# Softmax weights of attention units: broadcast by VectorE and turned, in place of two broadcast matmuls on TensorE

## The chip, the cores and the metric

One core of a Trainium2 chip. The metric is the device time of one execution in microseconds; before: median 2764.86 us of three runs (2764.49, 2764.86, 2767.98). The core's engines are TensorE (PE, its weight loads listed apart as PEld), VectorE (DVE), ScalarE (ACT), GpSimd (POOL) and SyncE (SP). Matmul results land in PSUM, in banks of 512 float32 columns.

## The reference, cut to what matters

Two transformer blocks in float32. The first has two layers over 512 latent and 256 context tokens, each with three attention mixers of 8 heads of width 64: A (global), B (a neighbourhood on a grid) and C (a sliding window with a sink logit per head). The second block has two layers over 512 tokens with, beside other mixers, a causal attention of 4 heads with forget decays. All of them end alike:

```python
def softmax_f32(s, dtype):
    return jax.nn.softmax(s.astype(jnp.float32), axis=-1).astype(dtype)

    def block(qi):
        s = jnp.einsum('bqhgd,bkhd->bhgqk', qi, k_all)
        p = softmax_f32(s, v_all.dtype)
        return jnp.einsum('bhgqk,bkhd->bqhgd', p, v_all)
```

Context tokens attend to context tokens alone, and only in the first layer of block one, since nothing reads them after it.

## The kernel before, in words

Attention works in units. A unit is one block of 128 queries for a pair of heads (e = 0 and 1). There are 136: in layer 0 of block one 16 latent and 8 context units for each of A, B and C, in layer 1 16 latent units each, and in block two 8 units in each of its two layers. Each unit goes through these steps; the line numbers are those of the profile:

- `scores_pe` (L494, in block two also L498 for the decays): TensorE computes the scores of both heads into PSUM. For scores wider than 512 columns, which fill two banks a head, it first waits for the exponentials of the unit before (`exp_done`); otherwise for those of two units before.
- `maxima_dve`: VectorE adds the mask and takes the row minimum of the negated scores: L574 writes the sink columns (mixer C), L579 adds the causal mask (block two), L590 adds mask and reduces in one, L585 reduces alone. Signal `max_ready`.
- `exponentials_act` (L670): ScalarE computes the exponentials and the row sums, head by head. Signal `exp_done`.
- `turn_probs_pe` (L519): TensorE turns the probabilities, 128 x 128 at a time, up to four into one bank; each bank is an event (`turned`).
- `turned_act` (L660) and `turned_dve` (L602): ScalarE copies the first two banks of a unit to SBUF, VectorE the third if there is one.
- `weights_dve` (L608): VectorE takes the reciprocal of the two row sums. Signal `weight_ready`.
- `outputs_pe`: TensorE waits until the output of the unit before has been taken (`y_done`) and for `weight_ready`, then spreads each head's 128 reciprocals over 64 partitions: one matmul a head whose stationary operand is the column of reciprocals broadcast to 64 columns and whose moving operand is the identity (L530). Behind it, event by event, come the products of the turned probabilities with the values (L540), each event behind its copy.
- `outputs_dve`: VectorE copies the spread weights to SBUF (L615) and multiplies the outputs by them (L626; in block two L620, a rounding L622 and the rest L624). Signal `y_done`.

No planner sets the order of these; it is written out. In block one the engines go step by step, with u the unit of the step and prev the one before: TensorE does scores(u), turn_probs(prev), outputs(prev), and turns of values (L550) where a new group of heads comes; VectorE does maxima(u), turned(prev), weights(u), outputs(prev), then copies of turned values (L635); ScalarE does its copies for prev, then the exponentials of u. In block two the same pieces are threaded through the projection tiles m = 9 to 15, by hand: for m = 10, for instance, TensorE does scores(U2), turn_probs(U1), the first two chunks of the projection (six products, L1952), outputs(U1), the other chunks; VectorE does maxima(U2), one tap of a convolution (L1538), weights(U2), outputs(U1), another tap.

Other lines named here: L1825, L1934 and L1952 are the large products of the blocks (fp32r in split halves), L1804 sums on TensorE for the modulation, L1392 its products on VectorE, L1773 the first modulation panels.

## Time and profile before

| | |
|---|---|
| median of the runs | 2764.86 us |
| the profiled execution: time, span | 2770.37 us, 2768.4 us |
| PE busy | 2541.0 us (92%), 14512 instructions |
| PEld busy | 2020.5 us (73%) |
| DVE busy | 1486.3 us (54%), 2630 instructions |
| ACT busy | 928.9 us (34%) |
| mean granted TensorE clock | 0.959 of full speed |

PE is matmuls and turns, PEld the weight loads, which overlap them. The starts of loads are recorded; the ends of matmuls are modelled. A float32 matmul is recorded as two instructions (two passes), a turn as one. The mixers of block one run from about 180 to 285, 405 to 485, 558 to 650, 960 to 1045, 1148 to 1207 and 1262 to 1337 us; the attention of block two from 1586 to 1650 and from 2207 to 2270 us.

### The profile page before, as it was taken

The page shows a single profiled execution, that of the slowest core. Times are in us where ns is not written, and L with a number is a line of the kernel's source. Part 1 is how long each engine was busy: PE and PEld are TensorE (multiplying, and loading weights), DVE is VectorE, ACT ScalarE, POOL GpSimd, SP SyncE. Part 2 cuts the span into 40 slices and gives each one's busy share as a digit, 9 for nine tenths or more (in the row PEclk, how much of TensorE's full clock was granted, in tenths as well). Part 3 has the DMA queues.
Part 4 walks back from the last instruction along what each step waited for, and adds up shares of the span by engine and source line. Part 5 has one row for each costly group of instructions (what it writes and reads, how often), then busy time and mean ns, then how long its engine had stood idle before and what let it go on. Part 6 is the DMA issues. An engine that isn't in the chain of part 4 may idle for free.

```text
span 2768.4 us, 38515 instructions
## 1 busy us (share of the span) xinstructions
PE 2541.0 (92%) x14512; PEld 2020.5 (73%) x14512; DVE 1486.3 (54%) x2630; ACT 928.9 (34%) x1682; POOL 487.0 (18%) x272
## 2 busy tenths in 40 slices
PE   5889999989997899997888898999998898999998
PEld 5656886767886568776777665788887665788886
DVE  4855875556623666574762775433333775433333
ACT  1335236253223253434333433322223333322221
POOL 1200120201234102210134423100002323100001
PEclk9979999999998899999998999999999899999998
DMA  6200341303312304330443211222223211223221
GB/s 247 101 27 1 115 152 39 122 2 138 141 59 89 122 2 169 113 115 20 149 144 111 84 54 41 89 92 94 104 81 103 71 54 46 86 91 98 101 84 67
DMA packets 64322, 250.49 MB, mean 90 GB/s; under 512 B 7803, under 2 KB 9339, under 8 KB 54661
## 3 DMA queue, kind: packets, MB, share of 16 engines
q1 hardware_dynamic: 59844, 234.31, 23.9%
q0 software_dynamic: 3776, 13.63, 1.5%
q8 instruction: 118, 1.93, 0.3%
q14 instruction: 72, 0.58, 0.1%
q10 hardware_dynamic: 512, 0.03, 0.0%
HBM read 243.72 MB, written 4.19 MB: 90 GB/s over the span
## 4 chain that ended last, share of the span: by engine, by line
PE 76%; DVE 8%; ACT 8%; issue 3%; DVEq 1%; POOL 1%; DMA 1%; ACTq 1%; SPq 0%; POOLq 0%
PE ps L1952 34%; PE ps L1825 16%; PE ps L1934 6%; PE ps L494 6%; PE ps L519 5%; ACT probs L670 4%; PE ps L540 2%; DVE projected L1538 2%; DVE probs L1392 2%; ACT probs_turned L660 2%; PE ps L1804 1%; PE ps L1773 1%; PE ps L530 1%; PE ps L550 1%; DVEq L1395 1%
## 5 line engine op out<-in xcount | busy, mean ns | idle before, releaser
L1952 PE MATMUL ps<-h_split,split_panels 128*128 128x512 f32 x3120 | 743.0, 398 | 16.1 <-DVE h_split L1513 13.5
L1952 PEld LDWEIGHTS ps<-h_split,split_panels 128*128 128x128 f32 x3120 | 590.4, 191 | 154.6 <-DVE h_split L1513 14.6
L1825 PE MATMUL ps<-h_split_first,split_panels_first 128*128 128x512 f32 x2880 | 568.4, 356 | 18.1 <-DVE h_split_first L1432 10.4
L1825 PEld LDWEIGHTS ps<-h_split_first,split_panels_first 128*128 128x128 f32 x2880 | 468.1, 191 | 103.0 <-issue 16.0
L879 POOL TENSOR_TENSOR split_panels_first<-panels_first,split_panels_first 128x1024 fp32r<-128x1024 f32 (+1 forms) x104 | 234.2, 2252 | 871.2 <-ACT split_panels_first L1010 871.2
L1392 DVE SCALAR_TENSOR_TENSOR probs<-modulation_panels,silu_c,probs 128x256 f32<-128x256 f32 x560 | 355.6, 651 | 34.3 <-issue 0.9
L1498 DVE TENSOR_TENSOR split_panels<-panels,split_panels 128x1024 fp32r<-128x1024 f32 (+2 forms) x168 | 190.0, 1131 | 304.4 <-ACT split_panels L1127 302.7
L1127 ACT ACTIVATE split_panels<-panels 128x1024 fp32r<-128x1024 f32 (+2 forms) x210 | 204.2, 974 | 343.1 <-PE ps L1952 341.6
L1952 PE MATMUL ps<-ffn_hidden_split,split_panels 128*128 128x512 f32 x1056 | 242.4, 392 | 0.0
L1952 PEld LDWEIGHTS ps<-ffn_hidden_split,split_panels 128*128 128x128 f32 x1056 | 198.6, 188 | 43.2
L670 ACT ACTIVATE probs<-ps,row_min 128x512 f32<-128x512 f32 (+7 forms) x272 | 187.8, 703 | 56.3 <-DVE row_min L585 41.9
L660 ACT COPY probs_turned<-ps 128x512 f32<-128x512 f32 (+1 forms) x240 | 128.9, 581 | 230.0 <-PE ps L519 230.0
L887 POOL TENSOR_TENSOR probs<-probs 128x512 f32<-128x512 f32 (+1 forms) x42 | 61.7, 1470 | 799.1 <-ACT probs L1134 784.1
L494 PE MATMUL ps<-qkv 64*128 64x256 f32 (+2 forms) x1056 | 152.2, 414 | 38.1 <-ACT probs L670 38.1
L519 PE MATMUL ps<-matrices,probs 128*128 128x128 f32 x1104 | 153.3, 283 | 4.9 <-ACT probs L670 4.9
L519 PEld LDWEIGHTS ps<-matrices,probs 128*128 128x128 f32 x1104 | 120.8, 143 | 46.5 <-issue 30.1
L1010 ACT ACTIVATE split_panels_first<-panels_first 128x1024 fp32r<-128x1024 f32 (+1 forms) x104 | 104.5, 1005 | 148.8 <-PE ps L1934 116.7
L1934 PE MATMUL ps<-gated_rounded,split_panels_first 128*128 128x512 f32 x576 | 145.4, 361 | 9.7 <-DVE gated_rest L1475 9.7
L494 PEld LDWEIGHTS ps<-qkv 64*128 64x128 f32 x1056 | 89.5, 198 | 84.6 <-ACT probs L670 56.5
L943 POOL TENSOR_TENSOR split_panels<-panels,split_panels 128x1024 fp32r<-128x1024 f32 x36 | 91.4, 2540 | 207.1 <-ACT split_panels L1127 207.1
L1051 ACT ACTIVATE qkv<-ps 128x512 f32<-128x512 f32 x38 | 36.6, 964 | 247.1 <-PE ps L1825 247.1
L1934 PEld LDWEIGHTS ps<-gated_rounded,split_panels_first 128*128 128x128 f32 x576 | 96.8, 191 | 26.5 <-issue 9.8
(222 smaller groups left out, 2641.8 us busy)
## 6 DMA issues: line engine op xcount, KB each, us to landing
modulation_panels<-in_ada SPq DMA_DIRECT2D x64, 1024.0 KB, 4.8
panels<-in_w SPq DMA_DIRECT2D x88, 512.0 KB, 3.2
panels_first<-in_in SPq DMA_DIRECT2D x72, 512.0 KB, 5.8
panels<-in_in SPq DMA_DIRECT2D x42, 512.0 KB, 3.3
panels_first<-in_out SPq DMA_DIRECT2D x32, 384.0 KB, 3.0
panels<-in_w SPq DMA_DIRECT2D x32, 384.0 KB, 3.0
panels<-in_w SPq DMA_DIRECT2D x32, 320.0 KB, 2.8
mixed_first<-in_ada SPq DMA_DIRECT2D x8, 1024.0 KB, 7.6
```

Of the source, the lines that this page charges most:

```text
L494: ins = nc.tensor.matmul(scores_at(u, e, 1024 if u["wide"] else 512)[:, col:col + z - a], u["q"][e], u["k"][e][:, a:z], start=True, stop=T ...
L519: ins = nc.tensor.transpose(bank(ev["bank"], at0, at0 + P), probs[:, u["i"] % 2, e, col:col + P], ident)
L660: nc.scalar.copy(probs_t[:, ev["slot"], 0:n], bank(ev["bank"], 0, n)).then_inc(pt_by_act, 1)
L670: nc.scalar.activation(probs[:, u["i"] % 2, e, 0:w], scores_at(u, e, w), ACT.Exp, bias=row_min[:, s:s + 1], scale=-1.0, accum_out=row_sum[ ...
L879: nc.gpsimd.tensor_tensor(flat1(n, 1), raw1[:, n % RAW1, 0:main_size(n)], flat1(n, 0).bitcast(F32), ALU.subtract).then_inc(rest1_done, 1)
L1010: A_(flat1(n, 0), raw1[:, n % RAW1, 0:main_size(n)], ACT.Copy).then_inc(rounded1, 1)
L1127: A_(flat(n, 0), raw[:, n % RAW, 0:panel_size(n)], ACT.Copy).then_inc(rounded, 1)
L1392: ins = V.scalar_tensor_tensor(out=to[:, i, :], in0=w[:, c, :], scalar=v, in1=to[:, i, :], op0=ALU.mult, op1=ALU.add)
L1498: V.tensor_tensor(flat(n, 1), raw[:, n % RAW, 0:panel_size(n)], flat(n, 0).bitcast(F32), ALU.subtract).then_inc(rest_done, 1)
L1825: ins = mm(at0, split1[:, s, w, c, :], hs1[:, h, c, lo:e], start=c == 0 and i == 0, stop=c == KC - 1 and i == 2)
L1934: ins = mm(bank(4 - 2 * j + o % 2, 0, e), split1[:, n % SPLIT1, w, c, :], u[:, uc, lo:lo + e], start=uc == 0 and i == 0, stop=uc == MIXC - ...
L1952: ins = mm(out, split[:, n % SPLIT, a, c - base, :], moving(b, c), start=first and i == 0 and j == 0, stop=last and i == len(chunks) - 1 a ...
```

## The change

Each reciprocal is now written 64 times into a 128 x 128 SBUF tile by VectorE (two copies with a broadcast source, a drain ahead of them), and TensorE turns that tile with one transpose into the place where the two matmuls wrote. The transpose stands directly behind the turns of the probabilities of the unit, with the waits for `y_done` and `weight_ready` ahead of it; `outputs_pe` keeps only the products with the values. There is one such tile, so VectorE waits until the unit before has been turned (a new semaphore, `weight_turned`). In block one nothing lies between the two functions on TensorE, in block two part of a projection tile does.

```diff
@@ -197,6 +197,7 @@
         row_sum = sb("row_sum", [P, 4])
         weight = sb("row_weight", [P, 4])
         y_weights = sb("weights_of_y", [P, P])
+        wide_weight = sb("wide_weight", [P, P])
         sinks = sb("minus_sinks", [P, DEPTH * HEADS])
         qn8 = sb("minus_q_norm_scaled", [P, DEPTH])
 
@@ -302,7 +303,7 @@
         band_in = [sem(f"band_in{v}") for v in range(3)]
         s_ready, max_ready, exp_done, weight_ready = (sem(n) for n in ("s_ready", "max_ready", "exp_done", "weight_ready"))
         turned, pt_by_act, pt_by_dve, values_taken = (sem(n) for n in ("turned", "pt_by_act", "pt_by_dve", "values_taken"))
-        pv_steps, y_done = sem("pv_steps"), sem("y_done")
+        pv_steps, y_done, weight_turned = sem("pv_steps"), sem("y_done"), sem("weight_turned")
         u_ready = sem("u_ready")
         out_half, out_ready = sem("out_half"), sem("out_ready")
         u_rounded, u_split = sem("u_rounded"), sem("u_split")
@@ -518,17 +519,15 @@
                 for at0, col, e, _ in places(ev):
                     ins = nc.tensor.transpose(bank(ev["bank"], at0, at0 + P), probs[:, u["i"] % 2, e, col:col + P], ident)
                 ins.then_inc(turned, 1)
-
-        def outputs_pe(pe, u, o):
-
             if u["i"] >= 1:
 
                 pe.wait_ge(y_done, u["u"] + o.u)
             pe.wait_ge(weight_ready, u["u"] + 1 + o.u)
-            s, b = 2 * u["i"] % 4, u["out_bank"]
-            for e in range(2):
-                nc.tensor.matmul(bank(b, P, 2 * P)[rows_of(e)], weight[:, s + e:s + e + 1].to_broadcast([P, HD]), ident,
-                                 start=True, stop=True, skip_group_check=True)
+            nc.tensor.transpose(bank(u["out_bank"], P, 2 * P), wide_weight[:, :], ident).then_inc(weight_turned, 1)
+
+        def outputs_pe(pe, u, o):
+
+            b = u["out_bank"]
             pe.wait_ge(values_taken, u["values_seen"] + o.w)
             for ev in u["events"]:
                 if ev["by"] == "act":
@@ -605,7 +604,14 @@
 
             s = 2 * u["i"] % 4
             dve.wait_ge(exp_done, 2 * u["u"] + 2 + o.u * 2)
-            nc.vector.reciprocal(weight[:, s:s + 2], row_sum[:, s:s + 2]).then_inc(weight_ready, 1)
+            nc.vector.reciprocal(weight[:, s:s + 2], row_sum[:, s:s + 2])
+            dve.drain()
+            if u["u"] >= 1:
+
+                dve.wait_ge(weight_turned, u["u"] + o.u)
+            for e in range(2):
+                ins = nc.vector.tensor_copy(wide_weight[:, HD * e:HD * e + HD], weight[:, s + e:s + e + 1].to_broadcast([P, HD]))
+            ins.then_inc(weight_ready, 1)
 
         def outputs_dve(dve, u, o):
```

## Rows read from the trace of the kernel before

**Rows 1.** The page's part 4, the whole span: share of the chain by line.

```profile
PE ps L1952 34%; PE ps L1825 16%; PE ps L1934 6%; PE ps L494 6%; PE ps L519 5%; ACT probs L670 4%; PE ps L540 2%; DVE projected L1538 2%; DVE probs L1392 2%; ACT probs_turned L660 2%; PE ps L1804 1%; PE ps L1773 1%; PE ps L530 1%; PE ps L55
```

**Rows 2.** Groups by line, engine, operation and shape, whole span.

```profile
L519 PEld LDWEIGHTS ps<-matrices,probs 128*128 128x128 f32 x1104 | 120.8, 143 | 46.5 <-issue 30.1 <-ACT probs L670 12.5
L530 PE MATMUL ps<-matrices,row_weight 128*64 128x128 f32 x544 | 60.5, 301 | 0.3
```

**Rows 3.** The same view, 500 to 2100 us.

```profile
L574 DVE COPY ps<-minus_sinks 128x1 f32<-128x1 f32 x80 | 8.8, 156 | 24.7 <-PE ps L494 24.7
L622 DVE CAST mixed_projected<-weights_of_y 128x128 fp32r<-128x128 f32 x8 | 1.8, 227 | 0.6
```

**Rows 4.** Timeline, a latent unit of mixer A: start, us, engine, line, operands.

```profile
223.48 0.17 DVE L608 RECIPROCAL row_weight<-row_sum 128x2 f32<-128x2 f32 x1 [1.03 <-ACT probs L670]
223.50 0.30 PEld L494 LDWEIGHTS ps<-qkv 64*128 64x128 f32 x4 [0.58 <-ACT probs L670]
223.56 0.27 DVE L615 COPY weights_of_y<-ps 128x128 f32<-128x128 f32 x1
224.99 1.29 PEld L519 LDWEIGHTS ps<-matrices,probs 128*128 128x128 f32 x12 [0.33 <-issue]
225.11 1.82 DVE L585 TENSOR_REDUCE row_min<-ps 128x1 f32<-128x768 f32 x2 [0.91 <-PE ps L494]
226.45 0.20 PEld L530 LDWEIGHTS ps<-matrices,row_weight 128*64 128x64 f32 x4 [0.17 <-issue]
226.61 1.39 PEld L540 LDWEIGHTS ps<-probs_turned,qkv 128*64 128x64 f32 x24
228.58 0.30 PEld L494 LDWEIGHTS ps<-qkv 64*128 64x128 f32 x4 [0.58 <-ACT probs L670]
```

**Rows 5.** Timeline, a band unit of mixer B, and the chain's piece for it.

```profile
448.24 0.86 PEld L519 LDWEIGHTS ps<-matrices,probs 128*128 128x128 f32 x8 [0.33 <-issue]
448.94 1.07 ACT L660 COPY probs_turned<-ps 128x512 f32<-128x512 f32 x2 [1.14 <-PE ps L519]
449.27 0.20 PEld L530 LDWEIGHTS ps<-matrices,row_weight 128*64 128x64 f32 x4 [0.17 <-issue]
449.64 0.45 PEld L540 LDWEIGHTS ps<-probs_turned,mixed_first 128*64 128x64 f32 x8 [0.17 <-issue]
...
449.34 0.37 PE ps L530 x4
```

**Rows 6.** Timeline, a latent unit of mixer C.

```profile
591.77 0.22 DVE L574 COPY ps<-minus_sinks 128x1 f32<-128x1 f32 x2 [0.49 <-PE ps L494]
```

**Rows 7.** Timeline, context units of mixer A, of B, and of C.

```profile
271.44 0.74 DVE L585 TENSOR_REDUCE row_min<-ps 128x1 f32<-128x256 f32 x2
272.39 0.48 ACT L670 ACTIVATE probs<-ps,row_min 128x256 f32<-128x256 f32 x1
...
442.39 0.73 DVE L585 TENSOR_REDUCE row_min<-ps 128x1 f32<-128x256 f32 x2
443.27 0.48 ACT L670 ACTIVATE probs<-ps,row_min 128x256 f32<-128x256 f32 x1
...
632.23 0.17 DVE L608 RECIPROCAL row_weight<-row_sum 128x2 f32<-128x2 f32 x1 [0.91 <-ACT probs L670]
633.15 0.76 DVE L585 TENSOR_REDUCE row_min<-ps 128x1 f32<-128x257 f32 x2
633.81 0.48 ACT L670 ACTIVATE probs<-ps,row_min 128x257 f32<-128x257 f32 x1
634.87 0.17 DVE L608 RECIPROCAL row_weight<-row_sum 128x2 f32<-128x2 f32 x1 [0.96 <-ACT probs L670]
```

**Rows 8.** Timeline, block two, the fifth unit of the first layer.

```profile
1621.14 0.20 PEld L519 LDWEIGHTS ps<-matrices,probs 128*128 128x128 f32 x2 [0.33 <-issue]
1621.31 1.24 PEld L1952 LDWEIGHTS ps<-h_split,split_panels 128*128 128x128 f32 x6
1621.50 0.29 DVE L624 TENSOR_TENSOR mixed_projected<-weights_of_y,mixed_projected 128x128 fp32r<-128x128 f32 x1
```

## The prediction

> **What bounds the kernel now.** First the page's chain by line, to see whose time counts: TensorE's large products lead it, the attention lines L494, L519, L540, the exponentials L670 and the copies L660 follow, and L530, the line that the change replaces, has 1% [rows 1]. Then the groups by line and shape, for the price of one instruction [rows 2, 3]. Then the timeline unit by unit, because a share says nothing of what a unit waits for. There are 136 units (L608 runs once in each): in block one 32 latent and 8 context units of mixer A, the same of B and of C, and in block two 8 per layer. The reader is to see that they fall into kinds with different last waits.
>
> *Mixer A, latent.* Period 5.08 us (L494 at 223.50 and 228.58). The next scores wait for the exponentials: the load of L494 at 228.58 sits 0.58 us idle behind ACT L670 [rows 4]. TensorE has time left over, so has VectorE (0.91 us before L585).
>
> *Mixer B, bands.* TensorE looks full and the chain names L530 with 0.37 us in each unit [rows 5]. Read the starts instead. L530's first load is at 449.27, L540's at 449.64, though the four loads of L530 take 0.20 us. In mixer A L540 starts 0.16 us behind L530 [rows 4]. What holds it in B is the ScalarE copy of the first turned bank: it starts at 448.94, and L540 0.70 us later. The first of its two copies takes about 0.59 us, and the rest is the signal. So the chain's 0.37 us is mostly a wait for ScalarE that the view books on TensorE.
>
> *Mixer C, latent.* As A, 8 to 10 turns; the smallest idle time of VectorE in the loop is 0.49 us, before L574 [rows 6].
>
> *Context units.* VectorE goes from unit to unit with one wait only, for the exponentials.
>
> *Block two.* Units are threaded between projection products; TensorE is the bound, and there every TensorE instruction counts.
>
> **The change, part by part.**
>
> *TensorE.* Removed per unit: two matmuls, recorded as 4 passes (544 records of L530 for 136 units), 0.05 us apart (4 loads in 0.20, the next line 0.16 to 0.21 us later). Added: one turn like L519's, one record each; 12 loads take 1.29 us, so 0.11 each [rows 2, 4]. That is a gain of 0.10 us where TensorE has no other wait, and not the 0.26 that the chain's 0.37 suggests.
>
> *Where the 0.10 counts.* A: TensorE waits for ScalarE afterwards, 0. B: nine turns end at about 448.24 + 0.97, with the 0.17 us of idle before another shape 449.38, still before 449.64: 0 [rows 5]. C: 0. Block two: all 16 units, 1.6 us gained.
>
> Those 0.17 us before L530 need a choice. They are there after L519 (128 x 128) and there is none between L530 and L540 (both 128 x 64), although both L530 and L540 stand behind waits [rows 4]. So I book it on the change of shape; the turn of the wide tile has L519's shape, and the number of such changes stays. The Trainium skill says the same (TensorEngine Tiling (Array Packing), Key Properties: changing the tiling mode drains TensorE). If each wait made the gap instead, the new wait inside a run of equal shapes would cost 16 x 0.17 = 2.7 us in block two; I keep that for the upper end.
>
> *VectorE.* Per unit: before, L608 takes 0.17 us and L615 starts 0.08 us behind its start. Now the reciprocal must end (0.17), a drain follows (+0.08: L585 starts that far behind the end of the two sink copies, with a drain between; ends 0 and 0.11), then two copies of 128 x 64. Such a copy is not in the trace. Below it lies the one-element copy L574: 0.16 us for one, 0.22 for two, a step of 0.065. Above it lies L615, 128 columns from PSUM, 0.27 with nothing overlapped. Near it lies L622, SBUF to SBUF, 128 columns in 0.23 [rows 2, 3]. I take a step of 0.12 us, the one-element step and half of L622's growth over 0.16, rounded up for the read of one repeated column. Added: 0.17 + 0.08 - 0.08 + 2 x 0.12 = **0.41 us per unit**; ends 0.30 and 0.70.
>
> The Trainium skill has a rule against this edit: VectorE: DVE Perf Modes, The DRAIN you can't avoid, says the next operation does not start until the pipe is empty, and advises fewer operations. Here L615 starts 0.08 us into a 0.17 us reciprocal, so for unheld neighbours the trace disagrees; by the rule the two copies would cost their full 0.2 us each and the addition would be about 0.57 us.
>
> *What hides the 0.41.* A latent: 0.91 us idle. C latent: 0.49. B bands: the first exponential waits for ScalarE's copies about 0.5 us longer than for the minimum. B context: L585 starts at 442.39, the exponential could start 0.46 later (one reduce and the signal; where L670 waits for L585 and nothing else this is what lies between them) but starts at 443.27, room 0.42. A context: 271.44 and 272.39, room 0.49 [rows 7]. So 0 in all of these, but B and C have only 0.01 to 0.08 us left: this cover is thin. The result y of the unit before is also 0.41 later; the turn that waits for it has until 0.4 us ahead of L540 in context units, enough.
>
> *C context.* Here there are the two sink copies as well. L585 at 633.15, exponential possible at 633.61, actual 633.81: room 0.20 [rows 7]. The loop reciprocal, outputs, sinks, minimum, exponentials, reciprocal takes 2.64 us (632.23 to 634.87) and becomes 2.64 + 0.41 - 0.20 = 2.85. Seven steps of this kind x 0.21 = **+1.5 us**.
>
> *The move past a part of a projection (block two).* The turn of the weights, and with it the waits for y and for the weights, now stands ahead of six products of L1952. What is queued behind the wait: those products, the outputs, everything else on TensorE. In seven of eight units y was ready long before. In the fifth unit (first of the second pair) it was not: its two turns load at 1621.14, the products at 1621.31, while L624, which gives y, starts at 1621.50 and ends at 1621.79 [rows 8]. Before, L530 came only behind the six products, when y was there. Now: TensorE arrives at 1621.31 - 4 x 0.10 = 1620.91. VectorE began this unit behind TensorE's scores, 0.3 earlier, adds 0.41, so y is there at 1621.90 and with the signal (0.05 to 0.1) at about 1621.97. Stall 1.05 us; the six products no longer fill that time. In the unit after it, by the same sum, y is there before the turns end. The next layer repeats this. Twice: **+2.1 us**. VectorE's lag grows by 0.41 in each later unit until it next waits for TensorE, behind the last unit; nothing on TensorE waits for it in between.
>
> *Sum.* C context +1.5, block two -1.6 + 2.1, everything else 0: **+2.0 us**, on the profiled execution 2770.37 to 2772.4. The median of the runs, 2764.86, lies 5.5 us below that execution; a difference carries over unchanged: **2766.9 us**. No measurement of this kernel tells less than 0.2% (5.5 us) from no change.
>
> **The rivals.**
>
> *The chain is right (faster).* L530 stands on it in 52 units: 36 in block one, 16 in block two. If each gave 0.37 - 0.11 = 0.26 us, 13.5 us would go: 2751 (2755 with the stall and mixer C's context units). For it: the chain's pieces join without gaps. Against it: the 0.70 us from ScalarE's copy to L540, in A's 12-turn unit longer only because L530 itself came late. Chance 8%.
>
> *VectorE becomes the loop (slower).* The price is the added time per unit; it decides as soon as that passes 0.42 to 0.49 us. At 0.57 (also the skill's rule): C context 7 x 0.37 = 2.6, B and A context 8 x 0.15 + 7 x 0.08 = 1.8, C latent half of 32 x 0.08 = 1.3, block two -1.6 + 2.4: +6.5 us, 2771.4. At 0.70: 3.5 + 3.7 + 3.4 + 1.1, about +11.7, 2776.6. For it: the copy is unseen, and cover is thin in three kinds. Against it: overlapped starts everywhere on VectorE. Chance 15%.
>
> *No stall in block two.* If the signal order leaves y ready (savings not realised ahead of it), the sum is -0.1 us: 2764.8. Chance 10%; the sign isn't measurable.
>
> *One turn is not one pass.* L519 has one record per turn, 1104 for 1104; with two, block two would lose its 1.6 us gain. 2%.
>
> **How the numbers follow.** The forecast's mechanism 65%, no stall 10%, VectorE 15%, the chain 8%, one pass 2%. VectorE at 0.57 passes 5.5 us just so, hence slower 12%, faster 8%, same 80%. The range: 2761.0 holds half-realised gains on the chain and the scatter of the runs (0.4 below to 3.1 above the median), 2772.0 the price of 0.57 us.
>
> **What would show it.** Right: L530 gone, 136 turns of 0.11 us; per unit two VectorE copies whose end puts L615 0.4 to 0.5 us behind the reciprocal's start; A still 5.08 us; L540 in B still 0.70 us behind ScalarE's copy; C context near 2.85 us; a stall of TensorE of about 1 us in the fifth unit of block two, named for L624. Wrong: B's units shorter by 0.2 us or more (then the chain was right); L574 of mixer C's latent units without idle time before it (then VectorE is the loop).

## The result, and the profile after

The changed kernel takes 2785.84 us (median of four runs, 2780.64 to 2786.09) against 2764.68 us beside it, a ratio of 1.0066 (95% interval 1.0051 to 1.0081). In a second set of runs (e5 below) it was 1.0068 (1.0051 to 1.0085). I forecast 2766.9 us and at most 2772.0: the kernel is slower by some 18 to 21 us and not by 2. The profiled execution took 2786.09 us, span 2784.1, mean granted clock 0.956.

The groups of the changed lines come first, in the form of [rows 2, 3] (busy us, mean ns | idle before and what ended it).

```profile
L613 DVE COPY wide_weight<-row_weight 128x64 f32<-128x64 f32 x272 | 40.6, 192 | 10.8 <-issue 1.0
L526 PEld LDWEIGHTS ps<-matrices,wide_weight 128*128 128x128 f32 x136 | 19.4, 143 | 13.9 <-DVE mixed_first L632 11.4 <-issue 2.0
L573 DVE COPY ps<-minus_sinks 128x1 f32<-128x1 f32 x80 | 8.8, 156 | 13.0 <-PE ps L495 11.3
```

The reader is to see one pass per turn (136 of L526, where L530 had 544), and that L573, the sink copy of mixer C, has 13.0 us of idle time in front of it (80 copies in sum) where it had 24.7 [rows 3]: the cover on VectorE is half used up. In mixer A's latent units the timeline shows the same (compare [rows 4]):

```profile
228.37 0.17 DVE L607 RECIPROCAL row_weight<-row_sum 128x2 f32<-128x2 f32 x1 [1.03 <-ACT probs L676]
228.61 0.30 DVE L613 COPY wide_weight<-row_weight 128x64 f32<-128x64 f32 x2
228.82 0.28 DVE L621 COPY weights_of_y<-ps 128x128 f32<-128x128 f32 x1
230.00 1.82 DVE L584 TENSOR_REDUCE row_min<-ps 128x1 f32<-128x768 f32 x2 [0.53 <-PE ps L495]
231.15 0.14 PEld L526 LDWEIGHTS ps<-matrices,wide_weight 128*128 128x128 f32 x1
231.45 0.85 PEld L539 LDWEIGHTS ps<-probs_turned,qkv 128*64 128x64 f32 x16 [0.17 <-issue]
233.46 0.17 DVE L607 RECIPROCAL row_weight<-row_sum 128x2 f32<-128x2 f32 x1 [1.04 <-ACT probs L676]
```

The copy of the spread weights starts 0.45 us behind the reciprocal where it was 0.08, so VectorE's addition is 0.37 us (forecast 0.41), the reduction's idle time goes from 0.91 to 0.53, and the period is 5.09, against 5.08. TensorE's band unit in mixer B:

```profile
447.10 1.07 ACT L666 COPY probs_turned<-ps 128x512 f32<-128x512 f32 x2 [1.14 <-PE ps L520]
447.23 0.14 PEld L526 LDWEIGHTS ps<-matrices,wide_weight 128*128 128x128 f32 x1
447.80 0.88 PEld L539 LDWEIGHTS ps<-probs_turned,mixed_first 128*64 128x64 f32 x16 [0.43 <-issue]
```

The products still start 0.70 us behind ScalarE's copy, as in [rows 5], and the turn now ends early enough that 0.43 us of idle time stands between: the chain's 0.37 us was a wait for ScalarE, as forecast.

Mixer C's context units:

```profile
631.92 0.17 DVE L607 RECIPROCAL row_weight<-row_sum 128x2 f32<-128x2 f32 x1 [0.76 <-ACT probs L676]
633.22 0.76 DVE L584 TENSOR_REDUCE row_min<-ps 128x1 f32<-128x257 f32 x2
633.68 0.48 ACT L676 ACTIVATE probs<-ps,row_min 128x257 f32<-128x257 f32 x1 [0.46 <-DVE row_min L584]
634.73 0.17 DVE L607 RECIPROCAL row_weight<-row_sum 128x2 f32<-128x2 f32 x1 [0.76 <-ACT probs L676]
```

That is 2.81 us per unit against 2.64 [rows 7]; the forecast was 2.85. Block two's fifth unit, against [rows 8]:

```profile
1627.23 0.20 PEld L520 LDWEIGHTS ps<-matrices,probs 128*128 128x128 f32 x2 [0.33 <-issue]
1628.03 0.29 DVE L630 TENSOR_TENSOR mixed_projected<-weights_of_y,mixed_projected 128x128 fp32r<-128x128 f32 x1
1628.45 0.14 PEld L526 LDWEIGHTS ps<-matrices,wide_weight 128*128 128x128 f32 x1 [1.02 <-issue]
```

The stall of 1.02 us is there (1.05 forecast), behind the line that I named (L624, now L630).

**Where the rest went.** For this I took the n-th product of TensorE (the weights' own left out) in both traces and compared the starts. The difference grows or falls as follows, always against a profile of the kernel before (us; a plus is time lost; "second ones" are e5 against e16; layers 0 and 1 of block two are given apart). 1.2 GHz, a granted clock of 0.5, is the lower of TensorE's two levels in these traces, 2.4 GHz (1.0) the upper:

| stretch of the kernel before | first profiles | second ones | what stands there |
|---|---|---|---|
| 120 to 637 | -3.8 | -3.6 | before has two stretches at 1.2 GHz, at 290 and 488, that after lacks; not the change's, see below |
| 637 to 651 | +2.0 | +1.9 | C's context units, +1.5, and the start of the next row's stretch |
| 651 to 656 | +2.1 | +2.2 | a new stretch at 1.2 GHz |
| 656 to 1370 | +1.6 | +1.8 | two longer such stretches, at 760 and 869 |
| 1370 to 1426 | +2.7 | +2.6 | input panels: a later transfer |
| 1426 to 1580 | +1.8 | +1.8 | a longer stretch at 1.2 GHz, at 1504 |
| block two's attention, layer 0 | -0.4 | -0.4 | stall +0.9, turns -0.8, a stretch at 1.2 GHz that ends earlier -0.5 |
| its tail, the convolution's sums | +3.3 | +3.7 | a new wait, +3.2 |
| 1656 to 2210 | -1.2 | +2.7 | a stretch at 1.2 GHz behind the tail (second profile) |
| attention and tail, layer 1 | +5.4 | +3.1 | the same wait; a stretch at 1.2 GHz behind it (first profile) |
| the rest | +2.0 | +0.3 | |

The rows come to 15.5 and about 16 us. The medians differ by 18 to 21; both profiled executions of the kernel before lay 3 to 6 us above its median. The first row is part of this: e2 and e9, which issue the kernel before's instructions in this part, have neither of the two stretches (-3.1 us), and e12, which issues the changed kernel's, has both (-0.6). So they come and go within one and the same stream, and that row is no gain of the change. Of the rows, only C's context units and the attention's stalls and turns were in my sum. The tail is the largest single wait. A tap is one `scalar_tensor_tensor` of VectorE, one term of the convolution; the sums over it are TensorE's. In the kernel before, by its second profile (e16), VectorE's last taps and GpSimd's subtractions of the input panels:

```profile
1644.30 2.90 DVE L1538 SCALAR_TENSOR_TENSOR projected<-conv_in,this_layers_vectors,projected 128x512 f32<-128x512 f32 x4
1647.10 2.38 POOL L943 TENSOR_TENSOR split_panels<-panels,split_panels 128x1024 fp32r<-128x1024 f32 x1 [7.72 <-ACT split_panels L1127]
1650.23 2.90 DVE L1538 SCALAR_TENSOR_TENSOR projected<-conv_in,this_layers_vectors,projected 128x512 f32<-128x512 f32 x4
1655.38 2.36 POOL L943 TENSOR_TENSOR split_panels<-panels,split_panels 128x1024 fp32r<-128x1024 f32 x1 [5.91 <-ACT split_panels L1127]
1655.68 1.88 PE L2110 MATMUL ps<-projected,matrices 128*128 128x512 f32 x4
```

Here the two engines take turns, four taps take 2.90 us, and the sums over the convolution (L2110) wait for nothing. (Earlier in the attention taps lie on subtractions before the change too: 16 of the 120 taps take over 1 us in the kernel before, 22 in the changed one.) After:

```profile
1653.72 2.44 POOL L949 TENSOR_TENSOR split_panels<-panels,split_panels 128x1024 fp32r<-128x1024 f32 x1 [7.80 <-ACT split_panels L1133]
1653.84 5.02 DVE L1544 SCALAR_TENSOR_TENSOR projected<-conv_in,this_layers_vectors,projected 128x512 f32<-128x512 f32 x4
1660.24 4.98 DVE L1544 SCALAR_TENSOR_TENSOR projected<-conv_in,this_layers_vectors,projected 128x512 f32<-128x512 f32 x4
1661.89 2.79 POOL L949 TENSOR_TENSOR split_panels<-panels,split_panels 128x1024 fp32r<-128x1024 f32 x1 [5.74 <-ACT split_panels L1133]
1665.28 0.30 PEld L2116 LDWEIGHTS ps<-projected,matrices 128*128 128x128 f32 x2 [3.26 <-DVE projected L1544]
```

VectorE's lag has laid the taps onto the subtractions; two groups of four take 5.0 us each, and TensorE's loads stand idle for 3.26 us, in layer 1 as well (2288.90). The Trainium skill has a rule on this, which my prediction did not weigh: GPSIMD Engine Reference, Key points, says that GpSimd shares its SBUF interfaces with VectorE and contends with VectorE's instructions that have two SBUF inputs. A tap is such an instruction, and this trace agrees (single taps last 0.735 to 2.883 us).

### The profile page after: what moved, and what is told of

The parts are those of the page before. It is cut to its first block, busy times and chain, and to the rows that moved or that the text cites. A ratio compares the mean times of both kernels' runs of the same rounds, so it can differ in the third digit from the quotient of the medians.

```text
span 2784.1 us, 38109 instructions
## 1 busy us (share of the span) xinstructions
PE 2533.5 (91%) x14104; PEld 2010.6 (72%) x14104; DVE 1538.3 (55%) x2902; ACT 929.9 (33%) x1682; POOL 488.4 (18%) x272
## 4 chain that ended last, share of the span: by engine, by line
PE 72%; DVE 10%; ACT 9%; issue 3%; DVEq 3%; DMA 1%; POOL 1%; ACTq 1%; SPq 0%; POOLq 0%
PE ps L1958 32%; PE ps L1831 16%; PE ps L1940 6%; PE ps L495 5%; ACT probs L676 4%; PE ps L520 4%; DVE projected L1544 3%; ACT probs_turned L666 2%; DVE probs L1398 2%; PE ps L539 2%; PE ps L1810 1%; PE ps L1779 1%; DVEq L1559 1%; PE ps L549 1%; PE ps L1892 1%
## 5 line engine op out<-in xcount | busy, mean ns | idle before, releaser
L1958 PE MATMUL ps<-h_split,split_panels 128*128 128x512 f32 x3120 | 742.8, 397 | 17.3 <-DVE h_split L1519 15.5
L1544 DVE SCALAR_TENSOR_TENSOR projected<-conv_in,this_layers_vectors,projected 128x512 f32<-128x512 f32 x120 | 125.8, 1071 | 4.5
```

Of the source, the lines that this page charges most:

```text
L1544: ins = V.scalar_tensor_tensor(out=conv[:, t, :], in0=src, scalar=w, in1=conv[:, t, :], op0=ALU.mult, op1=ALU.add)
L1958: ins = mm(out, split[:, n % SPLIT, a, c - base, :], moving(b, c), start=first and i == 0 and j == 0, stop=last and i == len(chunks) - 1 a ...
```

## The experiments

Ratios are to the kernel before on the same chip, with their 95% intervals. Theory: it is VectorE's added time, and most of it is lost where its lag meets GpSimd. The main rival: TensorE's early turn, with its waits, makes everything late.

**Block one only, block two only.** The new form where `u["extra"]` is false (e1) or true (e2), else the old:

```diff
+            if not (not u["extra"]):      # e2: if not (u["extra"])
+                nc.vector.reciprocal(weight[:, s:s + 2], row_sum[:, s:s + 2]).then_inc(weight_ready, 1)
+                return
```

> New form in block one only, block two as before. Theory (VectorE's lag meets GpSimd at the end of block two's attention, +3.1 us a layer, and mixer C's context units give +1.8): about +2 us over before, plus whatever the clock gives or takes. Rival (block one costs as much as block two): +8 to +12. Rival (the clock alone, any shift of the work): +5 or more here too.

> New form in block two only. Theory: the stall of TensorE ahead of L2116 in both layers, about 3 us each, and the low clock that may follow it: +6 to +14 us over before. Rival (the loss lies in block one): 0 to +2. The sum of this and of the block-one kernel should be the whole +21 if the two parts are independent.

1.0030 (1.0019 to 1.0042) and 1.0034 (1.0019 to 1.0048): by the medians +8.5 and +10.5 us. They add up to the whole, so neither block is free. In e1 the rows of the table for block one are there (C +2.1, the stretch behind it +1.7, the panels +3.5) and none of block two's; in e2 it is the other way round, with tails of +3.4 us each and a stretch at 1.2 GHz behind the first.

**VectorE's part alone, TensorE's part alone.** e3 keeps the old matmuls and lets VectorE write the wide tile for nothing; e4 turns the wide tile early, but VectorE writes it in the first unit only, so the weights of the other units are left out. In both VectorE no longer waits for `weight_turned`. Shown against the changed kernel, cut:

```diff
# e3, TensorE (the two matmuls stand in outputs_pe, as before)
-            nc.tensor.transpose(bank(u["out_bank"], P, 2 * P), wide_weight[:, :], ident).then_inc(weight_turned, 1)
+            for e in range(2):
+                nc.tensor.matmul(bank(b, P, 2 * P)[rows_of(e)], weight[:, s + e:s + e + 1].to_broadcast([P, HD]), ident,
# e4, VectorE
+            if u["u"] > 0:
+                nc.vector.reciprocal(weight[:, s:s + 2], row_sum[:, s:s + 2]).then_inc(weight_ready, 1)
+                return
```

> VectorE does the drain and the two wide copies in every unit, TensorE keeps its two broadcast matmuls in their old place; the wide tile is read by nobody. Theory (VectorE's added time is the cause): nearly the whole loss, +16 to +21 us over before, and the 3 us stall ahead of the convolution's sums stays. Rival (the early turn with its waits is the cause): 0 to +3 us, no such stall.

> TensorE as changed, one early turn in each unit, but VectorE writes the wide tile in the first unit alone, so the weights of the others are left out. Theory: no stall ahead of the convolution's sums, 0 to -3 us against before (0.1 us a unit in block two gained, the fifth unit's stall of about 0.6 us lost). Rival (the early turn is the cause): +6 to +20 us.

1.0045 (1.0028 to 1.0062) against 1.0006 (0.9996 to 1.0015). e3 has the C row (+1.5) and both tails (+3.5 each, beside +0.7 in layer 0's attention and +1.3 in layer 1's); e4 has neither, though it has the fifth unit's stall (0.94 us). That speaks for the theory. But e3 lacks the stretch at 1.2 GHz behind C and the later panels, so the two parts together do more than each alone.

**The changed kernel again**, without an edit.

> The changed kernel once more, beside its variants on one chip, with a second profile. If the 21 us are all work and waits, the ratio is again about 1.0065 to 1.008 and the stretches at the lower granted clock are those of the first profile (the one at 647 us above all). If a part of them is where the granted clock happens to fall, the ratio scatters between 1.003 (the 8 us that the stalls account for) and 1.008, and the stretches differ from the first profile. The tail of block two's attention costs 3 us per layer in either case.

2785.65 us, 1.0068 (1.0051 to 1.0085). The table's second column is its profile: all rows return but those at the tails, where the stretch at 1.2 GHz falls behind layer 0's tail here and behind layer 1's in the first profile.

**Block two's turn late (e6), and the same again (e13).**

```diff
 def outputs_pe(pe, u, o):
+            if u["extra"]:
+                turn_weights_pe(pe, u, o)   # the y_done and weight_ready waits and the transpose
```

> As the changed kernel, but in block two (which has two units per panel with further work behind) the turn of the wide tile stands back behind the six products of its unit, where its waits can't hold the probabilities' products. Theory (the early place costs only the stall of 1.05 us at the fifth unit of each layer, the tail is VectorE's): the fifth unit's stall is gone, the tail stall of 3 us per layer stays, in sum 1 to 2.5 us below the changed kernel. Rival (it is the early wait that makes everything late, VectorE's lag included): the tail stall goes too, 7 to 9 us below the changed kernel.

> As the changed kernel in everything (VectorE's two copies, the turn in one pass), but the turn and its two waits stand where the matmuls stood before, behind all of the step's probabilities' turns and ahead of the products. Since nothing stands between the two places within a unit, only the order of the wait for the values' copy changes. Theory: there is no difference in what TensorE waits for, so the time is that of the changed kernel within 2 us, fifth unit's stall included, and e11's loss of 6 us is the 64-column matmuls' own or scatter. Rival: the place matters, 3 to 6 us below the changed kernel.

1.0065 (1.0049 to 1.0082) and 1.0057 (1.0040 to 1.0073). What I wrote ahead of e13, that nothing stands between the two places, holds in block one only; in block two the six products do. So e13 issues the same order as e6, and is a repetition of it: eight runs, 2779.73 to 2786.56, a gain on the changed kernel of 0.3 to 3 us by the ratios. The two stalls do not explain it. The fifth unit's is gone, but the sixth unit has one in its place in each layer; in e13:

```profile
1631.71 2.44 DVE L628 CAST mixed_projected<-weights_of_y 128x128 fp32r<-128x128 f32 x1
1634.64 0.14 PEld L529 LDWEIGHTS ps<-matrices,wide_weight 128*128 128x128 f32 x1 [1.38 <-issue]
```

VectorE's rounding of y, 0.23 us in every unit of the changed kernel, takes 2.44 here beside a subtraction of GpSimd that starts 0.02 us before it, and TensorE's turn waits for that y. So layer 0's attention is no cheaper than in the changed kernel. Both tails stay (+3.7 us in each layer of e13, with TensorE's loads idle for 3.10): the early wait does not make VectorE late, and the rival falls.

**One copy for both heads.**

```diff
-            for e in range(2):
-                ins = nc.vector.tensor_copy(wide_weight[:, HD * e:HD * e + HD], weight[:, s + e:s + e + 1].to_broadcast([P, HD]))
+            nc.vector.tensor_copy(wide_weight[:, :].rearrange("p (e n) -> p e n", e=2),
+                                  weight[:, s:s + 2].unsqueeze(2).to_broadcast([P, 2, HD])).then_inc(weight_ready, 1)
```

> As the changed kernel, but VectorE writes both heads' 64 repeats with one copy instead of two. Theory (VectorE's added time per unit, 0.37 us, decides): some 0.19 us less per unit, so C's context falls from 2.82 to 2.72 us per unit (0.7 us in sum), and the tail stall of 3 us per layer falls, by between 0.19 times 8 units, 1.5 us, and all of it; in sum 2 to 6 us below the changed kernel. Rival (it is that VectorE waits at all, for its pipeline and for TensorE's turn of the tile before): no more than 0.5 us below.

1.0062 (1.0045 to 1.0079). A miss in two ways: the copy of the spread weights now starts 0.38 us behind the reciprocal instead of 0.45, so one copy saves 0.07 us and not 0.19, because two copies overlap; and the tail did not shrink with it (TensorE's loads wait 3.25 us in layer 0, with two copies 3.26). C's context did, to +0.8 us, which is 7 steps x (0.30 added - 0.20 of room) = 0.7 by the forecast's sum, and the stretch at 1.2 GHz behind it is gone.

**GpSimd's two subtractions cut to 8 columns: in the changed kernel (e8), in the kernel before (e9).**

```diff
                 for i in range(SPLIT, N_IN2):
+                    n = 8 if i in (17, 18) else panel_size(i)
-                    nc.gpsimd.tensor_tensor(flat(i, 1), raw[:, i % RAW, 0:panel_size(i)], flat(i, 0).bitcast(F32),
+                    nc.gpsimd.tensor_tensor(flat(i, 1)[:, 0:n], raw[:, i % RAW, 0:n], flat(i, 0)[:, 0:n].bitcast(F32),
```

> As the changed kernel, but of GpSimd's subtractions of the input panels 17 and 18 in each layer only the first 8 columns are done (the rest part of those panels is left out otherwise); these are the ones that run while VectorE does the convolution's taps at the end of block two's attention. Theory (the two engines slow each other and VectorE's lag has moved the taps onto the subtractions): four taps take 2.9 us again instead of 5.0, TensorE's wait for the convolution falls from 3.3 us to under 0.5, 5 to 6 us below the changed kernel. Rival (the lag alone makes the taps late): the taps may be short but the wait stays above 1.5 us, under 3 us below the changed kernel.

> The kernel before with the same cut of GpSimd's subtractions of input panels 17 and 18 as in e8 (their rest parts are left out but for 8 columns), as the control for it. Theory (before, these two subtractions fall between the bursts of taps and cost nothing): within 1.5 us of the kernel before, so that of the 10 us that the cut brought the changed kernel at least 8 are the overlap. Rival (the cut takes load off that stage whatever the kernel): 4 us or more below the kernel before.

The changed kernel falls to 2775.52 us, 1.0034 (1.0021 to 1.0047); the kernel before stays, 1.0002 (0.9993 to 1.0012). So up to 10 us, half of the loss, hang on two GpSimd instructions in each layer that cost the kernel before nothing. VectorE's taps in e8:

```profile
1651.55 0.28 POOL L950 TENSOR_TENSOR split_panels<-panels,split_panels 128x8 fp32r<-128x8 f32 x1 [7.79 <-ACT split_panels L1134]
1651.68 2.90 DVE L1545 SCALAR_TENSOR_TENSOR projected<-conv_in,this_layers_vectors,projected 128x512 f32<-128x512 f32 x4
1655.96 2.90 DVE L1545 SCALAR_TENSOR_TENSOR projected<-conv_in,this_layers_vectors,projected 128x512 f32<-128x512 f32 x4
1660.02 1.88 PE L2117 MATMUL ps<-projected,matrices 128*128 128x512 f32 x4
```

VectorE has all its added work here, but both groups take 2.90 us and TensorE waits for neither: at the tail the lag alone costs nothing, the overlap does. Of the difference between the profiles, 6.4 us are the two waits (2 x 3.2) and 2 to 3 a stretch at 1.2 GHz behind one of them (1.7 in the first profile, 3.0 in e5, none in e8). Another 1.6 lie in the row 1426 to 1580, ahead of the cut, where both kernels issue the same instructions; so the overlap, with the lower clock behind it, costs 8 to 9 us rather than 10.

**The two old matmuls kept beside the turn.**

```diff
+            for e in range(2):
+                nc.tensor.matmul(bank(u["out_bank"], P, 2 * P)[rows_of(e)], weight[:, 2 * u["i"] % 4 + e:2 * u["i"] % 4 + e + 1].to_broadcast([P, HD]), ident,
+                                 start=True, stop=True, skip_group_check=True)
             nc.tensor.transpose(bank(u["out_bank"], P, 2 * P), wide_weight[:, :], ident).then_inc(weight_turned, 1)
```

> As the changed kernel, but TensorE also issues the two old matmuls of 64 columns right ahead of the turn of the wide tile, in the same place (their result is overwritten). It adds 0.1 to 0.2 us of TensorE's work per unit and changes no wait. Theory (the stretch at 1.2 GHz at 647 us comes where TensorE does less between its waits): the stretch is gone and the time is 1 to 4 us below the changed kernel although TensorE does more. Rival (where the stretch falls has nothing to do with those matmuls): the stretch stays, and the time is the same or up to 3 us above.

1.0085 (1.0068 to 1.0102), about 5 us above the changed kernel. The stretch at 647 us is gone, as the theory had it (the row 651 to 656 is 0.0), and so are the later panels (1370 to 1426: 0.0), but the profile loses more elsewhere (+2.9 us in the first row, +6.0 in the row 656 to 1370, +3.5 in block two's attention of layer 0). Since e12 lacks the stretch at 647 as well, without these matmuls, its absence here does not show that they removed it. The time went the wrong way.

**The place alone.** The kernel before with its matmuls and their waits moved ahead of `outputs_pe`:

```diff
                 ins.then_inc(turned, 1)
-
-        def outputs_pe(pe, u, o):
-
             if u["i"] >= 1:
```

> The kernel before with its two matmuls of the weights and their two waits moved to right behind the probabilities, and nothing else: no wide tile, no added copies, no turn. Theory (the place is worth little but its waits cost at block two's fifth unit): that stall of 1.1 us appears in each layer, C's context, the 647 stretch and the tail are as before, in sum 0 to 3 us above the kernel before. Rival (the place is the gain that the copies ate): 1 to 3 us below the kernel before.

1.0023 (1.0013 to 1.0033), by the medians +5.8 us. The stall of 1.1 us that I expected in each layer is not what does it: in the fifth unit L527's load has 0.22 us idle in front of it, where TensorE comes 2.1 us later than in e4 (by the table's count). The traces lose 2.75 us in layer 0's attention and 2.6 in layer 1's, 0.3 to 0.4 in every unit. A unit of block two in e11, and the same one of the kernel before (e16):

```profile
1600.91 0.20 PEld L527 LDWEIGHTS ps<-matrices,row_weight 128*64 128x64 f32 x4 [0.17 <-issue]
1601.28 1.23 PEld L1953 LDWEIGHTS ps<-h_split,split_panels 128*128 128x128 f32 x6 [0.17 <-issue]
1602.86 0.64 PEld L541 LDWEIGHTS ps<-probs_turned,values_forgetting 128*64 128x64 f32 x12 [0.36 <-issue]
```

```profile
1606.54 1.24 PEld L1952 LDWEIGHTS ps<-h_split,split_panels 128*128 128x128 f32 x6
1608.13 0.20 PEld L530 LDWEIGHTS ps<-matrices,row_weight 128*64 128x64 f32 x4 [0.36 <-issue]
1608.30 0.69 PEld L540 LDWEIGHTS ps<-probs_turned,values_forgetting 128*64 128x64 f32 x12
```

Between equal shapes there is no idle time, before another shape 0.17 or 0.36 us. Put between the turns and the products, the 64-column matmuls add two such changes. The wide tile's turn has the shape of its neighbours and adds none: that choice of the prediction is shown, and with it most of why e4 loses less than e11 in this stage.

**GpSimd waits for the last tap.**

```diff
                     pool.wait_ge(rounded, i + 1 + l * PER2)
+                    if i == 18:
+                        pool.wait_ge(conv_done, 2 + l * 2)
```

> As the changed kernel with all its work, but GpSimd starts the subtraction of input panel 18 only when the last tap of the convolution is done, so it can't lie beside that tap. Theory (the overlap stretches the taps): the last tap takes 0.75 us instead of 2.83, TensorE's wait for the convolution falls from 3.3 to about 1.2 us in each layer, and the time is 2 to 5 us below the changed kernel. Rival (the rest part of panel 18 is then late by as much as the taps gain): TensorE waits for GpSimd behind the convolution's sums instead, within 1.5 us of the changed kernel.

1.0049 (1.0032 to 1.0066), some 5 us below the changed kernel.

```profile
1653.28 5.02 DVE L1546 SCALAR_TENSOR_TENSOR projected<-conv_in,this_layers_vectors,projected 128x512 f32<-128x512 f32 x4
1659.69 2.89 DVE L1546 SCALAR_TENSOR_TENSOR projected<-conv_in,this_layers_vectors,projected 128x512 f32<-128x512 f32 x4
1662.63 0.30 PEld L2118 LDWEIGHTS ps<-projected,matrices 128*128 128x128 f32 x2 [1.17 <-DVE projected L1546]
1662.66 2.37 POOL L951 TENSOR_TENSOR split_panels<-panels,split_panels 128x1024 fp32r<-128x1024 f32 x1 [7.05 <-DVE projected L1546]
```

With all the work done, moving one GpSimd instruction takes the last group of taps from 4.98 to 2.89 us and TensorE's wait from 3.26 to 1.17, as expected; the group before it still lies on a subtraction.

**A dearer write of the wide tile.** One reciprocal of 128 columns in place of the small one, the drain and the copies:

```diff
-            nc.vector.reciprocal(weight[:, s:s + 2], row_sum[:, s:s + 2])
-            dve.drain()
+            nc.vector.reciprocal(wide_weight[:, :].rearrange("p (e n) -> p e n", e=2),
+                                 row_sum[:, s:s + 2].unsqueeze(2).to_broadcast([P, 2, HD])).then_inc(weight_ready, 1)
```

> As the changed kernel, but VectorE takes the reciprocal of each row sum 64 times with one instruction of 128 columns, without the small reciprocal, the wait for its pipeline and the two copies. From the reciprocals of 2 and of 256 columns (0.17 and 1.72 us) that is 0.94 us, so some 0.86 us of added time per unit where the changed kernel has 0.37. Theory (the loss is VectorE's added time): C's context goes from 2.82 to 3.2 to 3.3 us per unit (3 us more), mixer B's context rises too (some 0.2 to 0.4 us over 16 units, 3 to 6 us), and in all 6 to 20 us above the changed kernel. Rival (the tail costs only by where the taps fall): with other phases the tail may even be free, and the time is no more than 3 us above the changed kernel.

2801.63 us, 1.0125 (1.0108 to 1.0142). It takes 0.95 us and adds 0.79 per unit; C's context costs +3.4 us. The loss grows with VectorE's time (0.37 us: +20, 0.79: +35), and more than half of it comes in block one, some 8 us ahead of the row 637 to 651, where most of the cover on VectorE that I had counted is now used up (6.1 us of idle time before the 80 sink copies, of 24.7).

**Three edits at once** (e6, e7 and e12 together).

> The changed kernel with three edits at once: block two's turn stands behind its unit's products (e6), VectorE writes both heads' repeats with one copy (e7), GpSimd's subtraction of panel 18 waits for the last tap (e12). If their gains add (about 2.6, 3.0 and 5.4 us by the medians), it is 9 to 12 us below the changed kernel and still 7 to 11 us above the kernel before. If they were the same gain three times, 5 to 6 us below the changed kernel. It beats the kernel before only if VectorE's 0.30 us per unit that remain cost nothing, which C's context speaks against.

2777.17 us, 1.0045 (1.0029 to 1.0062), 6 us below the changed kernel by the ratios and 8.5 by the medians: by the ratios hardly more than e12 alone, and nearer to the lower of the two expectations. C (+0.8), the panels (+4.2) and the tails (+1.7 each) remain.

**The kernel before again.**

> The kernel before once more, with a second profile. The ratio is 1 within 0.001. If the stretches at the lower granted clock follow the work, they fall where the first profile has them, with none at 647 us and none behind the convolution's sums, and their cost is 80 us within 2; if they fall by chance, the stretches of 3.4 us come elsewhere and the cost moves by as much as that of the changed kernel, 7 us.

2766.67 us, ratio 1.000 (0.999 to 1.001). All its stretches at 1.2 GHz between 160 us and 2100 start within 1 us of where the first profile has them (none at 647), but for one at 160 that starts 4 us later; they cost what they did (see the last section).

**The turn alone.** In the old place, VectorE writing the wide tile in the first unit only:

> TensorE turns the wide tile in one pass in place of its two matmuls, but where these stood before (in block two behind the unit's six products), and VectorE writes the wide tile in the first unit only, afterwards it makes only the small reciprocals (so the weights of the other units are left out). It is the most that the turn can bring, with a copy that costs nothing. Theory (C and B take nothing, block two's units save what TensorE saves, 0.1 us each, and e11's 6 us were the place): 1 to 3 us below the kernel before. Rival (TensorE's saving is hidden in block two too): within 1 us of the kernel before.

2771.68 us, 1.0017 (1.0008 to 1.0026): above the kernel before, which neither theory had. Block two's attention gains 1.2 us in layer 0 (0.4 of it where a stretch at 1.2 GHz ends earlier) and 0.9 in layer 1, each tail takes 0.6 back, and the row 1370 to 1426 loses 2.5 and the one behind it 1.9. With copies that cost nothing the turn wins nothing in either place (e4 1.0006, e17 1.0017).

**What these share: the panels.** The row 1370 to 1426, against e16, separates the kernels cleanly: +2.3 to +4.2 us in the ten other kernels in which block one has the turn and not the matmuls (e1, e4, e6 to e8, e12 to e15, e17), -0.3 to +0.2 in the five in which TensorE's matmuls stay there (e2, e3, e9 to e11), e10 with both among them. TensorE waits there for GpSimd, GpSimd for ScalarE, ScalarE for a transfer. SyncE's issues and ScalarE's splits in the changed kernel:

```profile
1408.71 0.33 SPq L840 DMA_DIRECT2D modulation_panels<-in_ada  x1
1409.08 0.43 SPq L834 DMA_DIRECT2D panels_first<-in_in  x1
1416.03 1.06 ACT L1016 ACTIVATE split_panels_first<-panels_first 128x1024 fp32r<-128x1024 f32 x1 [3.23 <-DMA panels_first<-in_in]
```

and in the kernel before (e16):

```profile
1404.84 0.33 SPq L834 DMA_DIRECT2D modulation_panels<-in_ada  x1
1405.21 0.43 SPq L828 DMA_DIRECT2D panels_first<-in_in  x1
1410.95 1.06 ACT L1010 ACTIVATE split_panels_first<-panels_first 128x1024 fp32r<-128x1024 f32 x1 [2.05 <-DMA panels_first<-in_in]
```

The same transfer behind the same neighbour is there 6.9 us after its issue, not 5.7. The traces show what lies in it. Beside the kernel's own queues there are queues of kind "instruction", and the packets of one of them, q8, follow TensorE's stream (the pages of the kernel before and after):

```profile
q8 instruction: 118, 1.93, 0.3%
q8 instruction: 115, 1.88, 0.3%
```

They number 115 wherever the turn stands in all units, 116 in e1, 119 in e10 and 118 in the kernels that keep the matmuls (e2 too, where only 16 units turn), and each is 16 KB: by this, it is TensorE's instructions that are loaded. With fewer instructions they are loaded at other times. In the eleven profiles of kernels with the turn in block one (two of the changed kernel; without e10, and without e14, whose stage lies elsewhere), such a packet starts 1.3 to 2.7 us behind the issue of this transfer, and of the transfer's 16 landings 15 come within 5.8 us and the last at 6.8 to 7.1. In the seven others it starts 6.1 to 8.0 us behind the issue, and the last landing comes at 5.6 to 5.8. The transfer at 1375 us is struck in the same way (7.0 to 7.8 us in the eleven, at most 6.0 in the six others that have it there). Over all 19 traces, 88 transfers of this form have a packet of q8 starting 0.6 to 4.5 us behind their issue and take 7.0 us in the median, the other 1070 take 5.7; one of the 88 is e10's, at 1395 us. So the shorter stream moves the loading of instructions into the transfer. That accounts for some 1.3 us each time; the rest of the row is in part a stretch at 1.2 GHz, at 1388 us in the first profile of the changed kernel and between 1414 and 1419 in seven others.

## Why the prediction was wrong

- **The step that failed** is the one that closes block two: "VectorE's lag grows by 0.41 in each later unit until it next waits for TensorE, behind the last unit; nothing on TensorE waits for it in between." The lag does grow, but the taps it delays run onto GpSimd's subtractions, four taps take 5.0 us instead of 2.9, and the convolution's sums on TensorE, right behind the attention, wait 3.2 us in each layer. e8 against e9 prices it at 8 to 9 us, with the lower clock behind it, and e12 confirms it with all the work done. I had not asked what stands ready at the next consumer (the convolution's sums behind the last tap are in none of my rows), nor what another engine does at the shifted time.
- **"A difference carries over unchanged"** and the costing of everything else at nothing were wrong too: 2 to 3 us at the panels (transfers that TensorE's instruction loading delays; e17 shows it without any VectorE work) and the stretches at 1.2 GHz. Up to 1580 us these cost about 5.5 (2.1 + 1.6 + 1.8), not counting the -3.8 of the first row, which is not the change's, and 2 to 3 more behind a tail.
- Right: VectorE's addition 0.37 us (forecast 0.41, ends 0.30 and 0.70); one record per turn; A and B unmoved, with L539 0.70 us behind ScalarE's copy; the fifth unit's stall 1.02 us (1.05) behind L630; the shape of the turn costing no extra 0.17 us (e11 against e4).
- C's context: right, +1.5 forecast. The stage's row has +1.9 to +2.0, but the 0.4 to 0.5 above 1.5 come after 648 us, in the stretch at 1.2 GHz; where there is no such stretch, e3 and e12 lose 1.5. By the sum itself the term at 0.37 us of addition is 7 x 0.17 = 1.2, so the match to the tenth is in part luck. e7 meets the same sum (0.7 against 0.8).
- Block two's saving of 1.6 us: within the attention of e17 it is there, 0.8 (without what the clock gives) + 0.9 = 1.7, but the tails take 2 x 0.6 back.
- The rivals: "the chain is right" is dead, as forecast. "VectorE becomes the loop" named the right engine for a wrong place: the room it watched (A, B, C latent) held, and its +6.5 us was still a third of the loss. The rule on the drain gave 0.57 us for the addition; 0.45 - 0.08 was measured, so unheld copies do overlap here. The prediction read that section too narrowly: the same section of the Trainium skill (VectorE: DVE Perf Modes, The DRAIN you can't avoid) says that a next operation that is not held starts earlier, and with this the trace agrees.

## What to carry to other kernels

Time added to an engine with idle time is not free because its own loop has room: follow the lag to the next place where it is not given back, and look at which other engine's work the delayed instructions will then lie beside, since two engines that took turns may now overlap and both slow down. Give a change of a fraction of a microsecond per unit a wide upper bound when long stages follow it, and run the control (the same cut in the kernel before) before believing an overlap's price. Fewer instructions on one engine also move the times at which its instructions are loaded, and a transfer that such a load falls into comes later (5.7 us became 6.9 here). Here none of the variants beat the kernel before.

## What the hardware showed that I had not expected

- A `scalar_tensor_tensor` of 128 x 512 float32 takes 0.74 us alone and 2.67 to 2.95 us when it starts beside GpSimd's `tensor_tensor` of 128 x 1024 (1.33 to 1.37 when it meets only a part of it); GpSimd's takes 2.4 alone and up to 2.94 beside it. The tap waits out nearly all of GpSimd's instruction. A cast of 128 x 128 with one SBUF input was held in the same way (0.23 us, in e13 2.44).
- A transfer of 512 KB (`panels_first`) behind another lands after 5.7 us, and after 7.0 when a 16 KB packet of TensorE's instruction queue falls into it; 15 of its 16 landings are then in time.
- The stretches at 1.2 GHz, away from the start of the program, return in nearly the same places in two profiles of one kernel: 80.7 and 80.1 us of cost before, 88.2 and 87.6 after (half of TensorE's busy time in them). But e9, whose stream is the kernel before's, costs 76.9 without those at 290 and 488. One stands at 647 us, directly behind C's context units, in both profiles of the changed kernel and in e1, e6, e8 and e13 (e14 at 662), and none in the kernel before or with one copy (e7) or the matmuls kept (e10). By windows, the kernel after (us, busy, then the granted clock and DMA):

```profile
640.00:647.00 7.00, 4.98 (x38) 2.81 (x36) 4.34 (x22) 3.83 (x14) 0.00 (x0) 1.00 0.00 0
647.00:654.00 7.00, 5.88 (x22) 4.66 (x23) 4.53 (x11) 1.79 (x2) 1.81 (x2) 0.53 0.35 95
```

  TensorE had been busy for 4.98 of 7 us ahead of it; before, 6.08 of 7 in the same window and no fall. But e3, busy for 5.09 us there, has no fall either, nor has e12, whose stream is the changed kernel's up to that point. So one stream can go both ways, and what decides stays open.
- Two copies of 128 x 64 take 0.19 us each by their records and 0.07 us more than one of 128 x 128.
